# A two-block model on one core: the second mixer's engine orders, the place of its p products, the pass order of the first gate tile, and the memory rows between two turnings

## The reference

```
for i in range(DEPTH):                       # DEPTH = 2
    mix = ssd_mixer(x, ...) if i % 2 == 0 else hgrn2_mixer(x, ...)
    h = layer_norm(ALPHA * x + mix, ...)
    h = layer_norm(ALPHA * h + sq_relu_mlp(h, w1[i], w2[i]), ...)
    x = h + sigmoid(h @ w_gate[i]) * (p[i] @ w_proj[i])
hgrn2_mixer: q, f, v, g = split(u @ w_in, 4); 8 heads of 128, chunks of 64 with a state;
             o = rms_norm(o) * silu(g), then o @ w_out
second block: x = mla_layer(x, mem, ...) with a memory of 256 rows:
             kv = rms_norm(mem) @ w_mem_kv, then attention, then a last norm
```

## Time and profile before

| | us |
|---|---|
| median of 3 timed runs | 2071.73 (2071.41 to 2072.03) |
| the profiled execution | 2071.23 |
| its span, first to last instruction | 2069.4 |
| TensorE busy | 1963.3 (95%) |
| VectorE busy | 1066.8 (52%) |
| ScalarE busy | 888.2 (43%) |
| GpSimd busy | 175.3 (8%) |
| mean granted TensorE clock | 0.974 |

### The profile page before, as it was taken

One profiled execution on the slowest core, in us unless ns is written; L12 is line 12 of the kernel. 1 busy time (PEld: TensorE's weight loads), 2 busy tenths in 40 slices (PEclk: granted clock), 3 DMA queues, 4 the chain that ended last, 5 costly groups with the idle time before them and its releaser, 6 DMA issues.

```text
span 2069.4 us, 26284 instructions
## 1 busy us (share of the span) xinstructions
PE 1963.3 (95%) x9450; PEld 1556.6 (75%) x9450; DVE 1066.8 (52%) x1899; ACT 888.2 (43%) x1758; POOL 175.3 (8%) x137
## 2 busy tenths in 40 slices
PE   7999999999999999999899599999999989989998
PEld 6788887868888887888888577888887765547763
DVE  4676666354434445567676654444436641045643
ACT  5665665253333234466576544233334520114430
POOL 0100110040000004001010040000003100001100
PEclk9999999999999999999999799999999999978999
DMA  5132124242322321333121014323222122210011
GB/s 190 41 103 61 41 82 147 75 146 82 117 87 82 121 82 41 82 82 82 41 76 47 21 63 145 119 81 104 98 81 102 51 67 89 65 41 1 0 41 41
DMA packets 116541, 161.30 MB, mean 78 GB/s; under 512 B 6021, under 2 KB 57059, under 8 KB 116451
## 3 DMA queue, kind: packets, MB, share of 16 engines
q1 hardware_dynamic: 115155, 155.38, 22.5%
q0 software_dynamic: 1296, 4.72, 0.7%
HBM read 157.98 MB, written 2.10 MB: 77 GB/s over the span
## 4 chain that ended last, share of the span: by engine, by line
PE 80%; DVE 9%; ACT 6%; issue 2%; DVEq 2%; DMA 1%; ACTq 1%; SPq 0%; POOLq 0%; POOL 0%
PE psum L902 40%; PE psum L677 10%; PE psum L1053 6%; PE psum L1213 4%; PE psum L642 4%; PE psum L865 3%; PE psum L1294 2%; PE psum L1085 2%; PE psum L1248 2%; PE psum L1261 2%; PE psum L826 1%; DVE w_lo L2137 1%; DVE z_lo L1927 1%; ACT fT L1351 1%; PE psum L1257 1%
## 5 line engine op out<-in xcount | busy, mean ns | idle before, releaser
L2137 DVE TENSOR_TENSOR w_lo<-slot,w_hi 128x512 fp32r<-128x512 f32 x304 | 213.8, 719 | 389.0 <-ACT w_hi L1520 389.0
L1520 ACT CAST w_hi<-slot 128x512 fp32r<-128x512 f32 x304 | 184.7, 621 | 453.6 <-PE psum L902 439.5
L902 PE MATMUL psum<-f_hi,w_hi 128*128 128x512 f32 x512 | 200.2, 391 | 1.5 <-ACT pT L1543 1.3
L902 PE MATMUL psum<-w_hi,hid_hi 128*128 128x512 f32 x512 | 199.6, 390 | 0.0
L902 PE MATMUL psum<-w_hi,hid_lo 128*128 128x512 f32 x512 | 199.3, 389 | 0.0
L902 PE MATMUL psum<-w_lo,hid_hi 128*128 128x512 f32 x512 | 199.2, 389 | 0.0
L902 PE MATMUL psum<-f_lo,w_hi 128*128 128x512 f32 x512 | 199.2, 389 | 0.0
L902 PE MATMUL psum<-f_hi,w_lo 128*128 128x512 f32 x512 | 199.2, 389 | 0.0
L642 PE MATMUL psum<-con,arena 128*128 128x128 f32 (+2 forms) x710 | 106.4, 289 | 20.4 <-ACT arena L1839 8.2
L642 PEld LDWEIGHTS psum<-con,arena 128*128 128x128 f32 (+2 forms) x710 | 87.4, 151 | 38.0 <-issue 12.3
L2633 POOL TENSOR_TENSOR res<-rn,gb 128x1024 f32<-128x1024 f32 x16 | 41.8, 2610 | 870.7 <-DVE rn L2125 870.7
(11 more groups left out here) (328 smaller groups left out, 4150.7 us busy)
## 6 DMA issues: line engine op xcount, KB each, us to landing
slot<-in_w_mlp SPq DMA_DIRECT2D x128, 512.0 KB, 5.8
slot<-in_w_ssd SPq DMA_DIRECT2D x32, 512.0 KB, 5.6
slot<-in_w_hgrn SPq DMA_DIRECT2D x32, 512.0 KB, 6.6
slot<-in_w_ssd_out SPq DMA_DIRECT2D x16, 512.0 KB, 6.1
slot<-in_w_gate SPq DMA_DIRECT2D x16, 512.0 KB, 5.4
gb<-in_w_ssd SPq DMA_DIRECT2D x8, 512.0 KB, 8.3
slot<-in_w_hgrn_out SPq DMA_DIRECT2D x8, 512.0 KB, 5.2
slot<-in_w_mla SPq DMA_DIRECT2D x8, 512.0 KB, 5.3
```

The lines of the kernel that those rows point to most:

```text
L902: m = pe.matmul(psum[:, bank[c], cols or slice(0, HALF)], a, m_, start=opens and k == 0 and n_pass == 0, stop=closes and k == KD - 1 and n ...
L1520: act.copy(w_hi[:, k, :], as_k(slot_of(stage, n))[:, k, :]).then_inc(high_made, 1)
L2137: dve.tensor_tensor(w_lo[:, k, :], as_k(slot_of(stage, n))[:, k, :], w_hi[:, k, :].bitcast(F32), ALU.subtract).then_inc(low_made, 1)
```

## The change

- **PE in a head.** Fill 3 is cut in halves: the first goes before level 5, the second between level 6 and the last level.
- **ScalarE in a head.** The next head's gates go before the scaling of the turned output; the casts of the next weights (groups 0 and 1) go before the next head's exponentials 0 and 1.
- **VectorE in a head.** Weight group 0, then the next head's levels 0 and 1, then the last predicated copy, then weight group 1, and only then the state copies; before, the state copies and the last copy came first and both groups last.
- **Last head.** Four of block 1's eight p products go into it (stages `proj1` with four, `proj1b` with four; the same weights are loaded twice, 1 MB each), with their four copies. Splits of the out weights and head outputs for k 0, 1, 2 go between its levels, 3 to 5 behind it. The out product's k 0 to 6 go before the turning of head 7's output, k 7 behind it. Banks and slots are given out anew.
- **Weights.** The loads of heads 0 and 1 wait for the gate's low parts and not for the next unit's begin.
- **First gate tile of each half, both blocks.** Eight passes f_hi x w_hi, then eight f_lo x w_hi, then eight f_hi x w_lo. The square root of tile 2 goes behind one cast and not three.
- **Block 1's first MLP part.** ScalarE copies two p tiles, does the last norm tile, then all eight casts, then two copies.
- **Memory rows.** Their mean squares go ahead of f_lo of tile 3, their scaling ahead of the half gates. PE turns normed tiles 0 and 1, multiplies the keys, then turns tile 2, values of memory tile 0, turning of tile 3, values of memory tile 1.

```diff
@@ -374,23 +374,24 @@
-def proj_banks(i, order):
-    banks.stage(f"proj{i}", [((h, t), order[(NHALF * t + h) % 4]) for t in range(NT) for h in range(NHALF)])
+def proj_banks(stage, tiles, order):
+    banks.stage(stage, [((h, t), order[(NHALF * t + h) % 4]) for t in tiles for h in range(NHALF)])
...
 norm_banks("norm00")
-proj_banks(0, (0, 2, 3, 1))
+proj_banks("proj0", range(NT), (0, 2, 3, 1))
 mlp_banks(0)
...
             + [("kt", 6), (("st", 0), 7), (("st", 1), 6), (("st", 2), 7), ("o", 6), ("ot", 7)], H_HEADS)
-banks.stage("hgrn_out", [((h, t), (4, 0)[h] + t) for h in range(NHALF) for t in range(NT)])
-norm_banks("norm10")
-proj_banks(1, (0, 1, 2, 3))
+proj_banks("proj1", range(2), (0, 1, 2, 3))
+banks.stage("hgrn_out", [((h, t), (0, 4)[h] + t) for h in range(NHALF) for t in range(NT)])
+norm_banks("norm10", 0)
+proj_banks("proj1b", range(2, NT), (4, 5, 6, 7))
 mlp_banks(1)
@@ -421,7 +422,7 @@
 order = [("ssd", 2 * S_GROUPS), ("ssd_out", 4), ("proj0", 1), ("mlp0", 4 * QUARTERS), ("gate0", 2), ("hgrn", H_HEADS),
-         ("hgrn_out", 2), ("proj1", 1), ("mlp1", 4 * QUARTERS), ("gate1", 2), ("mem", 1), ("cq", 1), ("ckv", 1), ("qm", 1),
+         ("proj1", 1), ("hgrn_out", 2), ("proj1b", 1), ("mlp1", 4 * QUARTERS), ("gate1", 2), ("mem", 1), ("cq", 1), ("ckv", 1), ("qm", 1),
          ("mgate", 2), ("uq", 1), ("ukv", 1), ("mla_out", 2)]
@@ -479,9 +480,13 @@
             sp.sem_inc(sig("slot_given"), 1)
-        elif stage == "hgrn_out" or stage == "hgrn" and per:
-            head = n if stage == "hgrn" else H_HEADS + n
+        elif stage == "hgrn" and not per:
+            sp.wait_ge(low_made, (split_units.index(u - 2) + 1) * KD)
+            sp.sem_inc(sig("slot_given"), 1)
+        elif stage == "hgrn" or stage == "proj1" or stage == "hgrn_out" and n == 0:
+            head = {"hgrn": n, "proj1": H_HEADS, "hgrn_out": H_HEADS + 1}[stage]
             sp.wait_ge(sig("cols_low"), 3 * (head - 1) + i * (3 * per))
@@ -594,9 +599,10 @@
             load_head(2 + n, j, 2)
+    load_proj("proj1", 1)
     for h in range(NHALF):
         load((P, KD, HALF), rows_cols(w_hgrn_out, 0, h * HALF, HALF), "hgrn_out", h)
-    load_proj(1)
+    load_proj("proj1b", 1)
     load_mlp(1)
@@ -954,9 +960,14 @@
-        proj(i, range(2))
-        last_turn()
-        proj(i, range(2, NHALF * NT))
+        if i == 0:
+            proj("proj0", 0, range(2), True)
+            last_turn()
+            proj("proj0", 0, range(2, NHALF * NT), False)
+        else:
+            proj("proj1b", 1, range(4, 6), True)
+            last_turn()
+            proj("proj1b", 1, range(6, NHALF * NT), False)
         input_ready(NT)
@@ -976,7 +987,25 @@
     def gate_tile(i, h, t):
-        gate_results(i, h, cs=(t,), begins=t == 0, ends=t == NT - 1)
+        if t:
+            gate_results(i, h, cs=(t,), begins=False, ends=t == NT - 1)
+            return
+        first = (part0[f"gate{i}"] + h) * KD
+        b = claim(f"gate{i}", (h, 0))
+        for n_pass, (f_part, w_part) in enumerate(((f_hi, w_hi), (f_lo, w_hi), (f_hi, w_lo))):
+            for k in range(KD):
+                if n_pass == 0:
+                    pe.wait_ge(high_made, first + (k + 1))
+                if n_pass == 2:
+                    pe.wait_ge(low_made, first + (k + 1))
+                m = pe.matmul(psum[:, b, :], f_part[:, k, 0:P], w_part[:, k, :], start=n_pass == 0 and k == 0,
+                              stop=n_pass == 2 and k == KD - 1)
+                if n_pass == 0 and k == 0:
+                    m.then_inc(blocks_begun, 1)
+                if n_pass == 1 and k == 0:
+                    m.then_inc(units_begun, 1)
+        m.then_inc(bank_full[b], 1)
@@ -1096,32 +1126,44 @@
+    def hgrn_out(h, **results):
+        times_parts("hgrn_out", h, lambda t, k: (o_hi[:, k, t * P:(t + 1) * P], o_lo[:, k, t * P:(t + 1) * P],
+                                                 w_hi[:, k, :], w_lo[:, k, :]),
+                    lambda t: ("hgrn_out", (h, t)), ready=None if h else lambda k: pe.wait_ge(sig("o_low"), k + 1), **results)
     def hgrn_core(par, i, first=False, last=False):
...
-        def fill(n):
+        def fill(n, *tts):
             if not last:
-                hgrn_project(*nxt, n)
+                hgrn_project(*nxt, n, *tts)
+        def tiles(js, begins=False):
+            if last:
+                proj("proj1", 1, js, begins)
...
         fill(1)
+        tiles(range(2), True)
         hgrn_level(par, i, 2)
...
         fill(2)
+        tiles(range(2, 3))
         hgrn_level(par, i, 4)
...
         m.then_inc(bank_full[b], 1)
+        fill(3, range(1))
+        tiles(range(3, 4))
         hgrn_level(par, i, 5)
-        fill(3)
         hgrn_level(par, i, 6)
+        fill(3, range(1, 2))
         hgrn_level(par, i, LEVELS)
@@ -1158,13 +1200,9 @@
     hgrn_core(1, 3, last=True)
+    hgrn_out(0, ks=range(KD - 1))
     hgrn_turn(H_HEADS - 1)
-    def hgrn_out(h, **results):
-        times_parts("hgrn_out", h, lambda t, k: (o_hi[:, k, t * P:(t + 1) * P], o_lo[:, k, t * P:(t + 1) * P],
-                                                 w_hi[:, k, :], w_lo[:, k, :]),
-                    lambda t: ("hgrn_out", (h, t)), ready=None if h else lambda k: pe.wait_ge(sig("o_low"), k + 1), **results)
-    hgrn_out(0)
+    hgrn_out(0, ks=(KD - 1,))
     last_turn = norm_turns("norm10", lambda t: hgrn_out(1, cs=(t,), begins=t == 0, ends=t == NT - 1))
@@ -1182,7 +1220,13 @@
     gate_tile(1, 1, 3)
-    last_turn = norm_turns("norm_mla", lambda t: None)
+    norms[0] += 1
+    def mla_turn(t):
+        turn_rows("norm_mla", rn, t, norm_ready, NT * 2 * DEPTH + t + 1)
+    mla_turn(0)
+    mla_turn(1)
     for m_ in range(MT):
@@ -1195,8 +1239,8 @@
         m.then_inc(bank_full[b], 1)
-    last_turn()
     for m_ in range(MT):
+        mla_turn(2 + m_)
         b = claim("memkv", ("v", m_))
@@ -1552,18 +1596,27 @@
             input_parts(stage, t - 1)
-        projected(i, 0)
-        projected(i, 1)
+        if i:
+            projected("proj1b", 1, 4)
+            projected("proj1b", 1, 5)
+            tile_out(stage, NT - 1, gain, bias)
+            split_high("mlp1", follows=False)
+            full("proj1b", (NHALF - 1, NT - 1))
+            projected("proj1b", 1, 6)
+            projected("proj1b", 1, 7)
+            return
+        projected("proj0", 0, 0)
+        projected("proj0", 0, 1)
         tile_out(stage, NT - 1, gain, bias)
-        projected(i, 2)
-        projected(i, 3)
-        split_high(f"mlp{i}", follows=False, ks=range(4))
-        projected(i, 4)
-        projected(i, 5)
-        split_high(f"mlp{i}", follows=False, ks=range(4, KD))
-        full(f"proj{i}", (NHALF - 1, NT - 1))
-        projected(i, 6)
-        projected(i, 7)
+        projected("proj0", 0, 2)
+        projected("proj0", 0, 3)
+        split_high("mlp0", follows=False, ks=range(4))
+        projected("proj0", 0, 4)
+        projected("proj0", 0, 5)
+        split_high("mlp0", follows=False, ks=range(4, KD))
+        full("proj0", (NHALF - 1, NT - 1))
+        projected("proj0", 0, 6)
+        projected("proj0", 0, 7)
@@ -1572,9 +1625,9 @@
         tile_out(stage, 0, gain, bias)
-        split_high(f"gate{i}", ks=range(3))
+        split_high(f"gate{i}", ks=range(1))
         root(n, 2)
-        split_high(f"gate{i}", ks=range(3, KD))
+        split_high(f"gate{i}", ks=range(1, KD))
         tile_out(stage, 1, gain, bias)
@@ -1623,6 +1676,10 @@
     def first_gate(i):
+        if i:
+            for m_ in range(MT):
+                act.wait_ge(sig("mem_ms"), m_ + 1)
+                act.activation(ms[:, m_, 1:2], ms[:, m_, 0:1], ACT.Sqrt).then_inc(sig("mem_root"), 1)
         for t in range(NT - 1):
@@ -1647,13 +1704,13 @@
     first_cols_high(0)
+    first_cols_high(1)
     gated(0, 1, 0)
     turn_high(0, 0)
-    first_cols_high(1)
+    first_cols_high(2)
     gated(0, 1, 1)
     turn_high(1, 0)
-    first_cols_high(2)
     gated(0, 1, 2)
@@ -1724,6 +1781,16 @@
+    def out_parts(ks):
+        for k in ks:
+            split_high("hgrn_out", follows=False, ks=(k,))
+            if k == KD - 1:
+                out_root(k)
+                out_turned(k)
+            wait_taken(act, "hgrn", "ot", k)
+            act.copy(o_hi[:, k, :], oT[:, k, :]).then_inc(sig("o_high"), 1)
     def hgrn_head(par, i, first=False, splits=True, last=False):
@@ -1736,20 +1803,28 @@
         ends(par, h)
+        if last:
+            out_parts(range(1))
         level_exps(h, 4)
+        if not last:
+            gates(1 - par, h + 1)
         if not first:
             out_turned(h - 1)
-        if not last:
-            gates(1 - par, h + 1)
         for n in (5, 6):
+            if last:
+                out_parts(range(n - 4, n - 3))
             level_exps(h, n)
+        if splits:
+            next_cols(par, i + 1, 0)
+            next_cols(par, i + 1, 1)
         if not last:
...
                 level_exps(h + 1, n)
-        if splits:
-            next_cols(par, i + 1, 0)
```

(58 more changed lines are left out.)

46 lines of the change are left out of this document (26 added, 20 removed).

## The result

The changed kernel takes **2021.99 us** (median of four runs, 2020.94 to 2025.46) where the kernel before takes 2071.77 (four runs beside it, 2071.41 to 2072.03): a ratio of 0.976, 95% interval 0.975 to 0.978. The forecast was 2031, with a range of 2019 to 2046. Both are used, because the difference between them is part of the answer.

A forecast was written before the change was run, and what follows sets the result against it. TensorE works nearly the whole span, so only closed holes or saved clock falls pay. Terms 2.75 + 3.85 + 4.15 + 12.1 + 4.5 + 1.6 + 11.9 = 40.85 off 2071.2 give 2030.4, forecast 2031 us, range 2019 to 2046.

The forecast's parts named there:

- First gate tiles: First gate tile of both blocks: earlier root and pass-by-pass order end row tile 1 sooner, 3.85 and 2.75 us.
- Head weights: Before the heads: earlier load of head 0 removes ScalarE's transfer wait and PE's 2.46 hole with its slow clock, 4.15 us.
- Heads: Heads 0 to 6: old holes covered, new 2.0 us hole before third state product, period 35.7, gain 12.1 us.
- The clock rule: PE's clock throughout: 1.7 us charged for a hole above 2.4 us, nothing below 2.1.
- the first rival: Heads: the new hole in each drops the clock, six heads lose 1.7 us each, 2041; chance 0.12.
- Last head: Last head to second out half: p tiles and out product fill holes, splits lengthen the chain, gain 4.5 us.
- Norm into MLP 1: Norm before block 1's MLP: four p tiles fewer, gain 3.3 less 1.7 for a 3.7 hole, 1.6 us.
- Memory rows and last norm: Last norm: mean squares fill a VectorE wait, PE's reordered turnings keep a 3.0 hole, gain 11.9 us.
- Later stages are only shifted: Stages after the edits: no gain, though the attention's 41 us half-clock stretch may move some 3 us either way.
- fill pays nothing: Last head: splits and p tiles lengthen its chain by all they save, heads win only 1 us each, 2042; chance 0.15.
- slower: Heads 0 to 6: clock falls at the state hole and stays down, 115 us lost less 41, 2145; chance 0.04.
- better: Fewer falls of the clock and a closed state hole: 3 x 1.7 + 4 us more, 2022; chance 0.10.

The follow-up runs named there:

- after_again: The changed kernel executed a second time for a second profile, nothing edited: 2020.54 us.
- gate_by_k: Changed kernel with the first gate tile back in the order k by k, three passes for each k: 2028.84 us.
- load_late: Changed kernel with the first load of head weights again behind the second gate's first matmuls: 2039.63 us.
- w1_behind: Changed kernel with VectorE's second weight part moved behind the state copies: 2016.43 us, ratio to before 0.9736.
- before_again: The kernel before the change executed a second time for a second profile, nothing edited: 2073.57 us.
- last_order: exps_first with the last head's splits of out weights and outputs and its token-wise k copy moved later: 2009.46 us, ratio 0.9693.
- exps_first: Changed kernel, heads only: levels 2 and 3 ahead of the last output's root and scaling, first state copy before copy 7, weight parts behind state copies: 2006.60 us.
- last_chain: exps_first with the last head reordered: ScalarE's exponentials to level 6 before root and values, PE and VectorE levels 2 to 6 first: 2001.11 us.
- mem_late: Changed kernel with the memory rows' mean squares, roots and scaling back behind VectorE's gates, PE's order kept: 2038.57 us.
- turn_first: Changed kernel with PE's turning of the last head's output back ahead of the whole out product: 2024.61 us.
- state_first: Changed kernel with the first state copy ahead of copy 7 and the second weight part behind the state copies: 2015.27 us.

## Why the prediction was right, and where its terms were wrong

The direction and the largest terms came true, and the new hole stands where it was forecast, 1.74 us long for 2.0 and with the cause that was given. The total came out 9 us too long, and in after_again, span against span, the gain is 50.7 for 40.85. Of these 9.9 us, 5.2 are the last row, which no edit of the change reaches. In the first profile the gain is 45.7, and that it comes nearer is luck: the heads win 4.7 less than forecast, the last row 4.9 more. The prediction's own sign of being wrong, heads above 37 us, did appear there: three heads take 37.37, though all of them together stand at a clock of 0.98. Term by term:

- **First gate tiles.** 3.85 forecast for block 0, 3.6 measured without a fall (2.5 with one); 2.75 for block 1, 2.5 measured. gate_by_k puts 1.6 of these to the pass order, by a fall of the clock that it avoids; the rest fits the 1.07 of the root. The prediction told this as waiting that 16 matmuls cover and named a lower clock before only for block 0, though block 1 has a fall there too, from 1601.2 to 1604.6.
- **Head weights.** 4.15 forecast, 4.3 measured. The term left out that the casts' new order leans on the load: with the late load it costs 3.1 (load_late, 44.0 for 40.9).
- **Heads.** 12.1 forecast, 12.3 measured where the clock stays up: period 35.73 (35.7), level 3 late by 0.66 (0.55), the hole where the prediction put it, 1.74 (2.0), released by the state copy. w1_behind confirms the cause that it gave, VectorE's weight parts ahead of the state copy. Of its own figures, 37.5 less 35.7 is 1.8 and not 1.85, which changes nothing.
- **The clock rule was the weak step.** "1.7 for a hole above 2.4 us, nothing below 2.1" charged nothing to six holes of 1.74. The first profile has three falls there, after_again none; the first rival, given 0.12, is true in part of the executions and costs 1.64 each time. The Trainium skill's rule behind that rival ("TensorE: Matmul & The Clock Gate", "A second HAM failure mode: psum-queue depth-cycling": short idle gaps between groups make the clock swing) is borne out by 11 of 36 holes, not by all; at 0.5 to 0.6 us (12 holes) there was no fall. The price, 1.7, was right; what was wrong was to read a threshold out of single holes. The trace of before already spoke against it, outside the stretches that were read: behind a hole of 1.57 us PE ran at half clock.

```profile
37.79 0.67 PE L677 MATMUL psum<-in_hi,ring 128*128 128x512 f32 x1 [1.46 <-DVE x_lo L1927]
...
1999.95 5.38 PE L642 MATMUL psum<-con,arena 128*128 128x128 f32 x32 [1.57 <-POOL arena L2676]
```

```profile
2000.60:2004.00 3.40, 3.40 (x19) 3.40 (x17) 1.38 (x2) 1.18 (x3) 0.00 (x0) 0.51 0.00 0
```

The hole before 37.79 has a fall behind it too, at 37.9. And both witnesses for "leaves it at 1.00" give way in before_again: one of its 1.44 us holes drops the clock (992.7), and so does the 2.06 us hole that was 2.04 (1235.1).

- **Last head.** 4.5 forecast, 4.7 and 5.2 measured, by another sum. The head's output product begins 28.4 us after head 6's (27.9 in after_again), for 25.4 before: 2.5 to 3.1 later, where the forecast put its end 4.2 later. The out product then ran behind it without a wait, as foreseen, and the hole at the turning is 2.25 (2.3). last_order shows that the splits in the chain, charged 1.2 and 1.3, cost 0.8 together in exps_first's order; in the changed kernel's own they were not taken out. The prediction did not cost the order of table loads, values and decay exponentials on ScalarE; last_chain, which puts root and values behind all the levels' exponentials and reorders PE and VectorE with them, takes 6.3 off exps_first's 25.7.
- **Norm into MLP 1.** 1.6 forecast, 3.2 measured. The step that failed is the 1.7 for the clock behind a hole of 3.7. The profiles show both cases. In the first two the clock already falls at the hole of 2.2 us ahead of turning 3, so it is the p tiles ahead of the wait that run slowly (5.11 for 3.60 us in the first, and the hole shrinks to 2.04), where it is free; in w1_behind, gate_by_k and load_late the p tiles run at full clock, the hole is 3.72, and the row is 366.6 to 367.5 for 365.0. The forecast had described the second case.
- **Memory rows and last norm.** 11.9 forecast, 14.7 measured. The third turning waits 1.70, not 3.0, and no fall follows it: 1.3 and the 1.7 charged are the difference. mem_late gives 5.8 of it to the rows.
- **"Later stages are only shifted"** was wrong by 4.9 to 5.2 us. The prediction said that the attention's half-clock stretch could end elsewhere, 3 us either way, and took 0. It was 10 to 14 us shorter, and no edit of the change reaches it. Over thirteen profiles the 8.2 us hole ahead of it is the same to 0.02 us, while the clock falls 1.5 to 4.2 us behind the hole's start. In seven it falls at 1.5 to 1.6 or 3.9 to 4.2 and the stretch lasts 27 to 31 us; in six it falls at 2.0 to 3.0 and the stretch lasts 41 to 44, and these six have the last row of 215.7 to 216.2, the seven 210.7 to 211.2. The changed kernel's edited variants show both, so the 5 us go with the moment of the fall and not with an edit; that the moment is the cause is not shown. Why both profiles of before fell in the longer kind stays open; its seven to nine runs beside each study lie within 4 us of each other, so it may do so always.

Of the rivals, "fill pays nothing" is refuted (turn_first, and the last head's row), "slower" and "no change" did not come near, and "better", 2022, named the sum that came out for another reason: it closed the state hole, which stands. In "slower", 7 x 16 is 112 and not 115, so its price is 2142 for 2145.

## What to carry to other kernels

When an order of work is turned round, list what now stands ahead of the instruction that another engine waits for: here one 1.21 us subtraction ahead of a 0.28 us copy cost 7 us over six heads, and moving both weight parts behind the state copies, with the exponentials ahead of the root, emptied all the heads' holes. Price an edit by the stretch it touches, cut at instructions that both kernels have, since whole times of one kernel spread by up to 9 us (2013.66 to 2022.46 in state_first), and two profiles of the changed kernel with the same waits differ by 5 us through the clock. Before a threshold is read out of a trace, look for every hole of that length in it. And look for the first long hole ahead of a stage of short dependent steps: closing it is worth the clock behind it too, here 10.6 us on top of its 7.9.

## What the runs showed of the hardware

- Equal holes do not have equal effects on the clock, and the longer hole is not the surer one. At 1.74 us, 11 of 36 dropped it to 1.2 GHz, for 3.4 us and 1.64 us of loss each. Of the holes of 1.57 us near the end of the kernel (1999.95 in before), one in each of the fourteen profiles, 11 of 14 were followed by a fall within 1 us; of those of 1.46 us near its start (37.79), 12 of 14 within 1.4 us; of the fourteen of 1.44 to 1.46 us in the heads of before, one. What sets these places apart was not tested. The Trainium skill ("TensorE: Matmul & The Clock Gate", "What's actually happening") says that the watch over TensorE's activity runs free of the kernel's start, so that the point of a transition varies; the two profiles of the same kernel agree.
- From within the 8.2 us hole on, the clock stayed at 1.2 GHz through 27 to 44 us of an attention stage in which PE works nearly without a pause at 2.4 GHz once the hole is away (32.52 of 33.00 us busy, clock 1.00). The length went with the moment of the fall, as above.
- A fall on work that only leads up to a wait for another engine was free (365.0 us for the row to gate norm 1 in five profiles of the changed kernel and its variants), and one that reaches behind the wait cost 1.6 to 2.4 us in the same place (366.6 to 367.5 in three).
